# Two transformer blocks on one core: the norms at the ends of the projections rearranged between PE, DVE and ACT

## The chip, the cores and the metric

The kernel runs on one core of a Trainium2 chip. The metric is the device time of one execution in microseconds, the median of three runs.

## What is computed

512 tokens of 1024 features go through two decoders in turn, each of two layers, all in float32. Cut to what the change touches:

```python
def rmsnorm(x, g):
    y = x * lax.rsqrt(jnp.mean(x * x, axis=-1, keepdims=True) + 1e-6)
    return y * g

# first decoder: two layers, then a closing norm
h = h + mixer(rmsnorm(h, norm1[i]), ...)          # attention, then @ w_out
h = h + conv_ffn(rmsnorm(h, ffn_norm[i]), ...)    # gelu(conv(g)) * u, then @ w_out
x = rmsnorm(h, final_norm)

# second decoder: two layers with a norm before and behind each half
mix = merged @ w_out[l]
x = x + rmsnorm(mix, norm_mix_post[l])
f = conv_gated_mlp(rmsnorm(x, norm_ffn_pre[l]), ...)
x = x + rmsnorm(f, norm_ffn_post[l])
```

The mixers are block, differential, dilated and latent attention in the first decoder, and axial attention, pooling and neighbourhood attention, gated and merged, in the second.

## The kernel before

**Layout.** Activations lie transposed: features on the 128 partitions, 512 tokens along the row, so the state `x` is eight tiles of 128x512. [...]

**Products.** Each float32 weight and activation is split into a high and a low part in `fp32r`; a product is three matmuls (L470 to L472: high by high, high by low, low by high). The high part of a normed `x` is `hh`, the rest is `hl`, both without the factor 1/rms: that factor multiplies the results (`rs`, 128x512, or `rsT`, one column per 128 tokens). GpSimd (POOL) splits the weights ahead of TensorE: a cast to `wh` (L450) and a subtraction for `wl` (L452), two buffers deep, fed by SyncE's DMAs.

**Order.** Every engine runs its own list, written by hand; semaphores join them, with counts worked out ahead by `counts` and `starts`. Output tiles of a projection go to the PSUM banks PA and PB in turn; bank PA is used again one tile later, once `pa_taken` has been raised.

**The end of a projection** has two forms.

- *out0, down0, out1, down1* (`x_add`, L1606): DVE adds the bank to the tile of `x` (L1613), which frees the bank; ACT makes `hh` from `x` times the next gain (L1040) and the square in `tmp` (L1041); DVE makes `hl` (L1298) and adds the square to `acc` (L1304). The norms before `up0` and `up1` are summed late, inside the next projection (`sum_acc`, one 128x512 product of ones with `acc`).
- *out2, down2* (`mix_copy`): ACT squares the bank (L1053), DVE copies it to `mix` (L1622) and adds the square (L1304).

**The five places where TensorE waits** are `norm_final` behind down1, and `norm_mp` and `norm_fp` behind out2 and down2 in each of two layers (I number the layers 0 and 1). `stat` (L506) sums `acc` over partitions into four columns of tokens (L511, four products of 2 columns each), ACT takes the root (L1027), DVE inverts it (L1277) and multiplies it into an identity, which gives 128x512 in `acc` (`factor`, L1278), and TensorE spreads it with a product of ones with that matrix (`spread`, L519) into bank O0. Then DVE renews `x` tile by tile: in `norm_post` with L1336 (`mix` by gain by O0), L1338 (the sum), in `norm_final` with L1325; ACT makes `hh` and the square, DVE `hl` (L1298), and TensorE starts the next projection tile by tile as `hl` comes: `up2` (`up` with `squared`), or `axial_kv` (L915 to L917 and PB), both with a 128x512 sum of ones with each square (L502). `moba_v` and `mla_cq` use `stat` and `spread` too, between products of a value projection.

Of the kernel before, what the change touches and what calls it, by code (L numbers as in the profile page):

```python
# [60 lines left out]
def counts(kind, seg=None, fin=0, mix=0):  # L61
    c = dict(e=SEGMENTS[seg][0] if seg else 0, a=0, b=0, u=0, g=0, v=0, n=fin, k=0, s=0, q=0, h=0, x=0, z=0,
             m=0, d=fin, r=0, st=0, df=0, pl=0, dr=0, dc=0)
    if kind == "x_in":
        c.update(s=1 + DT, q=DT, h=DT)
    elif kind == "v":
        c.update(v=1)
# [9 lines left out]
    elif kind == "mla_cq":  # L77
        c.update(a=1, b=1, d=fin)
# [4 lines left out]
    elif kind == "norm_post":  # L83
        c.update(q=DT, h=DT, x=DT, d=fin + DT)
# [49 lines left out]
    ("up1", counts("up1", "up1")), ("down1", counts("out", "down1")),  # L134
# [55 lines left out]
def build(nc, x_in, weights, consts, cols_in, lam_in, rel_in, rpb_in, strips_rel, strips_na, out):  # L190
    with ExitStack() as ctx:
# [110 lines left out]
        diag_ready, spread_ready = sem("diag_ready"), sem("spread_ready")  # L302
# [160 lines left out]
        def _(pe):  # L463
# [42 lines left out]
            def stat(b, spread_now=True):  # L506

                pe.wait_ge(acc_done, b["s"])
                pe.wait_ge(o_taken, b["u"] + 2)
                for t in range(QT):  # L510
                    last = mm(O1[:, 2 * t:2 * t + 2], acc[:, t * P:t * P + P], ones[:, 0:2], start=True, stop=True)  # L511
                last.then_inc(st_ready, 1)
                if spread_now:
                    spread(b)

            def spread(b):

                pe.wait_ge(diag_ready, b["n"] + 1)
                mm(O0[:, :], ones[:, :], acc[:, :], start=True, stop=True).then_inc(spread_ready, 1)  # L519
# [451 lines left out]
            def moba_stat():  # L971
                pe.wait_ge(table_in, 16 * NTABLE)
                stat(H("moba_v"), False)
# [14 lines left out]
            stat(b, False)  # L988
# [12 lines left out]
            stat(H("norm_final"))  # L1001
            with pe.Fori(0, LAYERS2) as l:
# [14 lines left out]
        def _(act):  # L1017
# [25 lines left out]
            def renew_out(b, gain_at, e_per=1):  # L1043

                with act.Fori(0, 4) as i:
                    for j, (bank, taken, key) in enumerate(((PA, pa_taken, "a"), (PB, pb_taken, "b"))):
                        if gain_at is None:
                            act.wait_ge(entry_done, b["e"] + e_per * (2 * i + j + 1) + 2)
                        else:
                            act.wait_ge(taken, b[key] + i + 2)  # L1050
                        act.wait_ge(acc_done, b["s"] + 2 * i + j + 1 - j)
                        if gain_at is None:
                            A(tmp[j][:, :], bank[:, :], ACT.Square).then_inc(sq_ready, 1)  # L1053
                        else:
                            renew(2 * i + j, gain_at, tmp[j][:, :])
# [938 lines left out]
```

## Time and profile before

| | us |
|---|---|
| median of 3 runs (lowest, highest) | 3264.05 (3263.01, 3266.23) |
| the profiled execution | 3260.93 |
| its span, first to last instruction | 3259.1 |
| TensorE busy (share) | 3105.8 (95%) |
| POOL busy | 1660.0 (51%) |
| DVE busy | 1481.7 (45%) |
| ACT busy | 788.6 (24%) |

A busy share of TensorE counts a matmul also while it waits in the pipeline or runs at half clock. The idle stretches lie at a few places; the timeline shows them, and the windows show the clock in them. The profiled execution is 1.8 us longer than its span and 3.1 us below the median.

### The profile page before, as it was taken

Reading aid. Unit: us, or ns where it says so; the run is one execution under the profiler, and the core shown is the slowest. Engines: PE = TensorE matmul, PEld = TensorE weight load, DVE = VectorE, ACT = ScalarE, POOL = GpSimd, SP = SyncE. Lnnn points to the kernel's source line nnn. Section 1 sums busy time; section 2 is a strip of 40 time slices with the busy share of each in tenths; the row PEclk is TensorE's granted clock in tenths of the full one; section 3 lists DMA queues with packets and bytes.
Section 4 is the critical chain, followed back from the end, with each engine's and each line's share of the span. In section 5 each row is a group of like instructions: output and inputs, shape, how many; then the busy total and the mean of one; then the engine's idle time right before and its main releaser. Section 6 shows DMA issues by size and latency. Waiting matters only on the chain.

```text
span 3259.1 us, 44842 instructions
## 1 busy us (share of the span) xinstructions
PE 3105.8 (95%) x14594; PEld 2441.7 (75%) x14594; DVE 1481.7 (45%) x2555; ACT 788.6 (24%) x1425; POOL 1660.0 (51%) x1254
## 2 busy tenths in 40 slices
PE   8998999999899999899999989998899999989997
PEld 6776888876678887667678868887667678868885
DVE  3246444332454433633533476631633433576622
ACT  2343221014322211243421122210142511122201
POOL 4324666662166666312346646665313256646674
PEclk9999999999999999889999989999889999999998
DMA  6251223321022233102312222232102322212232
GB/s 159 78 161 65 94 95 105 105 91 59 26 90 97 97 109 104 36 23 57 93 68 97 87 66 97 96 114 85 40 33 62 75 78 97 90 65 97 97 113 74
DMA packets 99595, 274.79 MB, mean 84 GB/s; under 512 B 38126, under 2 KB 38894, under 8 KB 99490
## 3 DMA queue, kind: packets, MB, share of 16 engines
q1 hardware_dynamic: 97328, 269.07, 25.8%
q10 hardware_dynamic: 2162, 4.36, 0.7%
q8 instruction: 61, 1.00, 0.1%
q14 instruction: 44, 0.36, 0.0%
HBM read 269.66 MB, written 11.54 MB: 86 GB/s over the span
## 4 chain that ended last, share of the span: by engine, by line
PE 71%; DVE 4%; issue 2%; ACT 1%; DVEq 0%; ACTq 0%
PE PA L470 11%; PE PA L471 10%; PE PA L472 10%; PE PB L470 8%; PE PB L472 8%; PE PB L471 8%; PE T L598 2%; PE O L604 2%; PE S L567 2%; PE O L699 1%; PE S L660 1%; PE O L502 1%; DVE hl L1298 1%; DVE tmps L1336 0%; PE PB L759 0%
## 5 line engine op out<-in xcount | busy, mean ns | idle before, releaser
L452 POOL TENSOR_TENSOR wl<-raw,wh 128x1024 fp32r<-128x1024 f32 (+2 forms) x416 | 1126.6, 2708 | 33.4
L449 POOL TENSOR_TENSOR zero<-zero 128x1 f32<-128x1 f32 x416 | 82.7, 199 | 1530.7 <-PE PA L472 799.0
L470 PE MATMUL PA<-hh,wh 128*128 128x512 f32 x1392 | 566.2, 407 | 30.4 <-DVE hl L1298 11.4
L471 PE MATMUL PA<-hl,wh 128*128 128x512 f32 x1392 | 550.1, 395 | 0.0
L472 PE MATMUL PA<-hh,wl 128*128 128x512 f32 x1392 | 549.6, 395 | 0.0
L450 POOL CAST wh<-raw 128x1024 fp32r<-128x1024 f32 (+2 forms) x416 | 476.8, 1146 | 0.0
L470 PEld LDWEIGHTS PA<-hh,wh 128*128 128x128 f32 x1392 | 265.7, 191 | 139.8 <-issue 65.8
L470 PE MATMUL PB<-hh,wh 128*128 128x512 f32 x896 | 358.5, 400 | 0.0
L472 PE MATMUL PB<-hh,wl 128*128 128x512 f32 x896 | 350.4, 391 | 0.0
L471 PE MATMUL PB<-hl,wh 128*128 128x512 f32 x896 | 350.2, 391 | 0.0
L472 PEld LDWEIGHTS PA<-hh,wl 128*128 128x128 f32 x1392 | 266.3, 191 | 57.6
L471 PEld LDWEIGHTS PA<-hl,wh 128*128 128x128 f32 x1392 | 266.4, 191 | 54.0 <-issue 2.2
L1074 ACT ACTIVATE probs<-biased,stats 128x512 f32<-128x512 f32 (+2 forms) x240 | 155.2, 647 | 408.6 <-PE T L598 226.3
L1631 DVE SCALAR_TENSOR_TENSOR tmps<-S,cols,tmps 128x511 f32<-128x511 f32 (+1 forms) x264 | 197.9, 750 | 39.6 <-DVE tmps L1631 19.8
L470 PEld LDWEIGHTS PB<-hh,wh 128*128 128x128 f32 x896 | 169.1, 189 | 47.5 <-issue 14.4
L472 PEld LDWEIGHTS PB<-hh,wl 128*128 128x128 f32 x896 | 168.7, 188 | 36.0
L471 PEld LDWEIGHTS PB<-hl,wh 128*128 128x128 f32 x896 | 169.1, 189 | 33.7 <-issue 1.2
L598 PEld LDWEIGHTS T<-ident,probs 128*128 128x128 f32 x792 | 98.8, 148 | 72.5 <-issue 37.3
L1170 ACT ACTIVATE T<-tmps 128x512 f32<-128x512 f32 x88 | 53.0, 602 | 391.7 <-DVE tmps L1631 391.7
L1298 DVE SCALAR_TENSOR_TENSOR hl<-x,cols,hh 128x512 fp32r<-128x512 f32 (+1 forms) x80 | 129.3, 1622 | 39.0 <-ACT hh L1040 38.8
L470 PE MATMUL PA<-acth,wh 128*128 128x512 f32 x352 | 137.4, 390 | 0.0
L598 PE MATMUL T<-ident,probs 128*128 128x128 f32 x792 | 136.3, 288 | 0.8 <-ACT probsT L1080 0.8
(285 smaller groups left out, 4928.0 us busy)
## 6 DMA issues: line engine op xcount, KB each, us to landing
raw<-in_w_up SPq DMA_DIRECT2D x176, 512.0 KB, 3.4
raw<-in_w_down SPq DMA_DIRECT2D x64, 768.0 KB, 4.2
raw<-in_w_merge SPq DMA_DIRECT2D x48, 768.0 KB, 4.2
raw<-in_w_out SPq DMA_DIRECT2D x32, 512.0 KB, 3.4
strips_na<-in_rpb SPq DMA_DIRECT2D x1, 7620.0 KB, 32.0
raw<-in_w_pool SPq DMA_DIRECT2D x12, 512.0 KB, 3.4
raw<-in_w_na_qk SPq DMA_DIRECT2D x12, 512.0 KB, 3.5
raw<-in_w_na_v SPq DMA_DIRECT2D x8, 512.0 KB, 3.5
```

Source lines behind the costliest of these rows:

```text
L449: nc.gpsimd.tensor_tensor(zero[:, :], zero[:, :], zero[:, :], ALU.add)
L450: nc.gpsimd.tensor_copy(wh[s][:, 0:width], raw[s][:, 0:width]).then_inc(w_head, 1)
L452: nc.gpsimd.tensor_tensor(wl[s][:, 0:width], raw[s][:, 0:width], wh[s][:, 0:width].bitcast(F), ALU.subtract).then_inc(w_split, 1)
L470: mm(dst, h_, rh, start=first, stop=False)
L471: mm(dst, h_, rl, start=False, stop=False)
L472: return mm(dst, l_, rh, start=False, stop=last)
L567: mm(SB[t % 2][:, 0:L], q_sb[r, qt * P:qt * P + P], k_sb[r, 0:L], start=True, stop=True).then_inc(s_ready, 1)
L598: last = nc.tensor.transpose(TB[t % 2][:, k * P:k * P + P], probs[t % 2][:, k * P:k * P + P], ident[:, :])
L604: last = mm(OB[t % 2][:, 0:dv], probsT[t % 2][:, k * P:k * P + P], values(k), start=(k == 0), stop=(k == L // P - 1))
L1074: A(probs[t % 2][:, 0:L], biased[t % 2][:, 0:L], ACT.Exp, scale=-1.0, bias=mn[:, t % 8:t % 8 + 1], accum_out=den[:, t % 8:t % 8 + 1]).then ...
L1298: STT(out=tile(hl, j), in0=tile(x, j), scalar=cols[:, bass.ds(gain_at + j, 1)], in1=tile(hh, j).bitcast(F), op0=ALU.mult, op1=ALU.subtract ...
L1631: ins = STT(out=dst[:, lo:hi], in0=src[:, lo - d:hi - d], scalar=w(k), in1=dst[:, lo:hi], op0=ALU.mult, op1=ALU.add)
```

## The change

1. **Late norms** (norm_final, norm_mp, norm_fp). `stat_last` takes the place of `stat`: TensorE sums `acc`, which now holds seven squares only, and then adds the eighth straight from `tmp[1]` into the same PSUM columns. `x_sum` and `mix_copy` leave out DVE's last addition.
2. **Factor and spreading** (all seven uses). DVE only inverts; the multiplication into an identity is gone. `spread` is four products of 128 columns, whose stationary operand is a column of `rsT` repeated 128 times, and whose moving one is the identity.
3. **Products that nothing reads** (`turning`, 128x512, identity by `causal`, into bank T0): (1, 1, 2) in norm_final, (0, 1, 3) in the others, before the last square, before the spreading and behind it.
4. **The sum in its bank** (out0, down0, out1). DVE adds `x` into the bank; `hh`, `hl` and the square are made from the bank, and ACT copies the bank to `x` at the end. Only that copy frees the bank.
5. **down1** no longer makes `hh` and `hl`; the squares are of `x` (`x_sum`, `square_out`).
6. The 128x512 sums inside `up0`, `up1`, `up2` and `axial_kv` stay.

```diff
 def counts(kind, seg=None, fin=0, mix=0):
...
-        c.update(a=4, b=4, s=1 + DT, q=DT, h=0 if mix else DT)
+        c.update(a=4, b=4, s=DT if mix else 1 + DT, q=DT, h=0 if mix else DT, xs=0 if mix else DT)
...
-    ("up1", counts("up1", "up1")), ("down1", counts("out", "down1")),
+    ("up1", counts("up1", "up1")), ("down1", counts("out", "down1", mix=1)),
...
+            def token_sums(src, first, last):
+
+                for t in range(QT):
+                    out_ = mm(O1[:, 2 * t:2 * t + 2], src[:, t * P:t * P + P], ones[:, 0:2], start=first and t == 0,
+                              stop=last and t == QT - 1)
+                if last:
+                    out_.then_inc(st_ready, 1)
...
+            def turning(times):
+
+                for _ in range(times):
+                    mm(T0[:, :], ident[:, :], causal[:, :], start=True, stop=True)
+
+            def stat_last(b, turns):
+
+                pe.wait_ge(acc_done, b["s"])
+                pe.wait_ge(o_taken, b["u"] + 2)
+                token_sums(acc, True, False)
+                turning(turns[0])
+                pe.wait_ge(sq_ready, b["q"])
+                token_sums(tmp[1], False, True)
+                turning(turns[1])
+                spread(b)
+                turning(turns[2])
+
+            def spread(b):
+
+                pe.wait_ge(inv_ready, b["n"] + 1)
                 for t in range(QT):
-                    last = mm(O1[:, 2 * t:2 * t + 2], acc[:, t * P:t * P + P], ones[:, 0:2], start=True, stop=True)
-                last.then_inc(st_ready, 1)
-                if spread_now:
-                    spread(b)
-
-            def spread(b):
-
-                pe.wait_ge(diag_ready, b["n"] + 1)
-                mm(O0[:, :], ones[:, :], acc[:, :], start=True, stop=True).then_inc(spread_ready, 1)
+                    last = mm(O0[:, t * P:t * P + P], rsT[:, t:t + 1].to_broadcast([P, P]), ident[:, :], start=True, stop=True)
+                last.then_inc(spread_ready, 1)
...
-            stat(H("norm_final"))
+            stat_last(H("norm_final"), (1, 1, 2))
...
-                stat(H("norm_mp", l))
+                stat_last(H("norm_mp", l), (0, 1, 3))
...
-                stat(H("norm_fp", l))
+                stat_last(H("norm_fp", l), (0, 1, 3))
...
+            def renew_out(b, gain_at):
+
+                with act.Fori(0, 4) as i:
+                    for j, (bank, taken) in enumerate(((PA, pa_taken), (PB, pb_taken))):
+                        n = 2 * i + j
+                        act.wait_ge(xs_ready, b["xs"] + n + 1)
+                        A(tile(hh, n), bank[:, :], ACT.Copy, scale=cols[:, bass.ds(gain_at + n, 1)]).then_inc(hh_ready, 1)
+                        act.wait_ge(h_ready, b["h"] + n + 1)
+                        act.wait_ge(acc_done, b["s"] + 2 * i + 1)
+                        A(tmp[j][:, :], bank[:, :], ACT.Square).then_inc(sq_ready, 1)
+                        A(tile(x, n), bank[:, :], ACT.Copy).then_inc(taken, 1)
...
             def factor(b):
 
-                chain_at(b["d"])
                 dve.wait_ge(std_ready, b["n"] + 1)
-                link(v.reciprocal(rsT, rsT))
-                TT(acc[:, :].rearrange("p (t n) -> p t n", t=QT),
-                   ident[:, :].rearrange("p (a n) -> p a n", a=1).to_broadcast([P, QT, P]),
-                   rsT.rearrange("p (t a) -> p t a", a=1).to_broadcast([P, QT, P]), ALU.mult).then_inc(diag_ready, 1)
+                v.reciprocal(rsT, rsT).then_inc(inv_ready, 1)
...
                 clear(b)
                 with dve.Fori(0, 4) as i:
+                    for j, bank in enumerate((PA, PB)):
+                        n = 2 * i + j
+                        dve.wait_ge(entry_done, b["e"] + e_per * (n + 1) + 2)
+                        TT(bank[:, :], tile(x, n), bank[:, :], ALU.add).then_inc(xs_ready, 1)
+                        dve.wait_ge(hh_ready, b["h"] + n + 1)
+                        STT(out=tile(hl, n), in0=bank[:, :], scalar=cols[:, bass.ds(gain_at + n, 1)],
+                            in1=tile(hh, n).bitcast(F), op0=ALU.mult, op1=ALU.subtract).then_inc(h_ready, 1)
+                        add_squares(b, n, tmp[j][:, :])
+
+            def x_sum(b, e_per):
...
+                        TT(tile(x, n), tile(x, n), bank[:, :], ALU.add).then_inc(taken, 1)
+                        if j < adds:
+                            add_squares(b, n, tmp[j][:, :])
+
+                with dve.Fori(0, 3) as i:
+                    both(i, 2)
+                both(3, 1)
```

The order of TensorE's list at `norm_fp`, behind the last product of down2 (`acth` by `wl` into bank PB; O is O1 in the narrow sums, O0 in the spreading; T is T0; `stats` holds `rsT`; a number after x repeats the row). Before:

```order
L472 MATMUL PB<-acth,wl 128x512
L855 REGISTER_ALU
L855 COMPARE_AND_BRANCH
L508 REGISTER_ALU
L511 MATMUL O<-ones,acc 128x2 [waits o_taken,acc_done]
L511 MATMUL O<-ones,acc 128x2 x3
L519 MATMUL O<-acc,ones 128x512 [waits diag_ready]
```

With the change (line numbers of the new file):

```order
L878 COMPARE_AND_BRANCH
L527 REGISTER_ALU
L509 MATMUL O<-ones,acc 128x2 [waits o_taken,acc_done]
L509 MATMUL O<-ones,acc 128x2 x3
L531 REGISTER_ALU
L509 MATMUL O<-ones,tmps 128x2 [waits sq_ready]
L509 MATMUL O<-ones,tmps 128x2 x3
L523 MATMUL T<-causal,ident 128x512
L541 MATMUL O<-ident,stats 128x128 [waits inv_ready]
L541 MATMUL O<-ident,stats 128x128 x3
L523 MATMUL T<-causal,ident 128x512 x3
```

The narrow sums are now eight products with the second wait in their middle, and four products that nothing reads stand around the spreading. `norm_mp` has the same rows; `norm_final` has one such product ahead of the second wait too, and two at the end.

ACT's list in the loop of out0, one tile (bank PA). Before:

```order
L1051 ISA [waits pa_taken]
L1040 ISA [waits acc_done]
L1040 REGISTER_ALU
L1040 ACTIVATE hh<-x,cols 128x512
L1041 ACTIVATE tmps<-x 128x512
```

With the change:

```order
L1072 ISA [waits xs_ready]
L1072 ACTIVATE hh<-PA,cols 128x512
L1073 REGISTER_ALU
L1074 REGISTER_ALU [waits h_ready]
L1075 ACTIVATE tmps<-PA 128x512 [waits acc_done]
L1076 REGISTER_ALU
L1076 ACTIVATE x<-PA 128x512
```

ACT reads the bank three times instead of `x` twice, the second time only behind DVE's `hl`, and the bank is free when the third is done.

## Rows read from the trace of the kernel before

**Rows 1.** The page, part 2: TensorE clock granted in 40 slices of 81.5 us, tenths

```profile
PEclk9999999999999999889999989999889999999998
```

**Rows 2.** Timeline at the first norm_mp: start us, us, engine, line, out<-in [idle before]

```profile
1881.91 0.60 ACT L1053 ACTIVATE tmps<-PB 128x512 f32<-128x512 f32 x1 [4.69 <-PE PB L472]
...
1882.53 1.28 ACT L1027 ACT_TABLE_LOAD   x1
...
1883.27 2.82 DVE L1304 TENSOR_TENSOR acc<-acc,tmps 128x512 f32<-128x512 f32 x1
...
1886.15 1.86 PE L511 MATMUL O<-ones,acc 128*128 128x2 f32 x8 [4.27 <-DVE acc L1304]
...
1888.05 0.26 ACT L1027 ACTIVATE stats<-O,eps 128x4 f32<-128x4 f32 x1 [4.24 <-PE O L511]
...
1889.31 2.07 PE L519 MATMUL O<-acc,ones 128*128 128x512 f32 x2 [1.29 <-DVE acc L1278]
...
1891.55 0.75 DVE L1336 SCALAR_TENSOR_TENSOR tmps<-mix,cols,O 128x512 f32<-128x512 f32 x1 [2.30 <-PE O L519]
...
1895.13 0.79 PE L470 MATMUL PA<-hh,wh 128*128 128x512 f32 x1 [3.75 <-DVE hl L1298]
...
1907.41 0.50 PE L470 MATMUL PA<-hh,wh 128*128 128x512 f32 x1 [0.18 <-DVE hl L1298]
```

**Rows 3.** Windows after norm_fp, layer 0: PE, PEld, DVE, ACT, POOL busy, PEclk, DMA

```profile
2279.10:2294.00 14.90, 14.90 (x50) 12.16 (x50) 12.69 (x19) 8.04 (x14) 0.00 (x0) 0.50 0.01 4
```

**Rows 4.** Timeline at norm_final, last tile of down1 to the next projection

```profile
1296.79 0.72 ACT L1040 ACTIVATE hh<-x,cols  x1 [13.63 <-DVE x L1613]
...
1305.82 1.41 DVE L1325 SCALAR_TENSOR_TENSOR x<-x,cols,O 128x512 f32<-128x512 f32 x2 [2.17 <-PE O L519]
...
1308.24 0.47 PE L915 MATMUL S<-wh,hh 128*128 128x128 f32 x1 [2.46 <-DVE hl L1298]
...
1335.57 0.79 PE L470 MATMUL PA<-hh,wh 128*128 128x512 f32 x1
```

**Rows 5.** Timeline after norm_fp of layer 0: first product of axial_kv, first of pool

```profile
2279.10 0.47 PE L915 MATMUL S<-wh,hh 128*128 128x128 f32 x1 [3.81 <-DVE hl L1298]
...
2309.00 0.79 PE L470 MATMUL PA<-hh,wh 128*128 128x512 f32 x1
```

**Rows 6.** Timeline of two products on PB, five 128-row blocks apart, at full clock

```profile
1319.06 0.45 PE L470 MATMUL PB<-hh,wh 128*128 128x512 f32 x1
...
1333.52 0.45 PE L470 MATMUL PB<-hh,wh 128*128 128x512 f32 x1
```

**Rows 7.** Timeline at the last norm_fp: end of down2, start of the renewal

```profile
3234.08 0.60 ACT L1053 ACTIVATE tmps<-PB 128x512 f32<-128x512 f32 x1 [14.21 <-PE PB L472]
...
3241.57 0.75 DVE L1336 SCALAR_TENSOR_TENSOR tmps<-mix,cols,O 128x512 f32<-128x512 f32 x1 [2.29 <-PE O L519]
```

**Rows 8.** Timeline at full clock: the narrow statistics (mla_cq) and a 128x512 sum (up1)

```profile
678.81 0.95 PE L511 MATMUL O<-ones,acc 128*128 128x2 f32 x8
...
940.88 1.02 PE L497 MATMUL O<-acc,ones 128*128 128x512 f32 x2
```

**Rows 9.** Timeline: a table load and the activation behind it, dilated attention

```profile
732.79 1.28 ACT L1074 ACT_TABLE_LOAD   x1 [4.76 <-DVE stats L1375]
...
734.09 0.40 ACT L1074 ACTIVATE probs<-biased,stats 128x128 f32<-128x128 f32 x1
```

**Rows 10.** Two lines: ns min/median/max, first and last start, forms

```profile
L1658 DVE TENSOR_TENSOR T<-T,tmps x88: 699/700/700, 323.2 to 3118.0; 128x512 f32<-128x512 f32 x88
...
L1304 DVE TENSOR_TENSOR acc<-acc,tmps x64: 677/680/2880, 270.5 to 3235.4; 128x512 f32<-128x512 f32 x64
```

**Rows 11.** Timeline: two tiles of out1 on bank PA, DVE

```profile
905.15 0.69 DVE L1613 TENSOR_TENSOR x<-x,PA 128x512 f32 x1 [0.71 <-PE PA L472]
...
907.05 2.23 DVE L1298 SCALAR_TENSOR_TENSOR hl<-x,cols,hh  x1 [1.21 <-ACT hh L1040]
...
916.04 0.69 DVE L1613 TENSOR_TENSOR x<-x,PA 128x512 f32 x1 [0.71 <-PE PA L472]
```

More of the change, by code:

```diff
@@ L66, in counts @@
     elif kind == "v":
-        c.update(v=1)
+        c.update(v=1, f=fin)
     elif kind == "q0":
@@ L972, in moba_stat @@
                 pe.wait_ge(table_in, 16 * NTABLE)
-                stat(H("moba_v"), False)
+                stat(H("moba_v"))
             v_projection(H("moba_v"), between=(None, moba_stat, lambda: spread(H("moba_v"))))
@@ L1225, in _ @@
             renew_out(H("out1"), CAT["ffn_norm1"])
-            sum_root(H("up1")); up(H("up1"), ACT.Gelu); renew_out(H("down1"), CAT["final"])
+            sum_root(H("up1")); up(H("up1"), ACT.Gelu); square_out(H("down1"), 2, True)
             b = H("norm_final")
@@ L1330, in norm_post @@
                 factor(b)
+                chain_at(b["d"])
                 dve.wait_ge(spread_ready, b["n"] + 1)
@@ new lines, in x_sum, with both @@
+            def x_sum(b, e_per):
+                clear(b)
+                def both(i, adds):
+                    for j, (bank, taken) in enumerate(((PA, pa_taken), (PB, pb_taken))):
+                        n = 2 * i + j
+                        dve.wait_ge(entry_done, b["e"] + e_per * (n + 1) + 2)
+                        TT(tile(x, n), tile(x, n), bank[:, :], ALU.add).then_inc(taken, 1)
[4 more added lines that the diff above has]
+                both(3, 1)
@@ L1617, in mix_copy, with both @@
             def mix_copy(b):
                 clear(b)
-                with dve.Fori(0, 4) as i:
+                def both(i, adds):
                     for j, (bank, taken) in enumerate(((PA, pa_taken), (PB, pb_taken))):
-                        dve.wait_ge(sq_ready, b["q"] + 2 * i + j + 1)
-                        v.tensor_copy(tile(mix, 2 * i + j), bank[:, :]).then_inc(taken, 1)
-                        add_squares(b, 2 * i + j, tmp[j][:, :])
+                        n = 2 * i + j
+                        dve.wait_ge(sq_ready, b["q"] + n + 1)
+                        v.tensor_copy(tile(mix, n), bank[:, :]).then_inc(taken, 1)
+                        if j < adds:
+                            add_squares(b, n, tmp[j][:, :])
@@ L1625, in conv @@
+                with dve.Fori(0, 3) as i:
+                    both(i, 2)
+                both(3, 1)
             def conv(dst, src, col, taps, last):
@@ L1796, in _ @@
             x_add(H("out1"), 1, CAT["ffn_norm1"])
-            up(H("up1"), CAT["conv1"], False); x_add(H("down1"), 2, CAT["final"])
+            up(H("up1"), CAT["conv1"], False); x_sum(H("down1"), 2)
             norm_final(H("norm_final"), CAT["final"], CAT["mix_pre"])
```

41 lines of the change are left out of this document (17 added, 24 removed).

## The prediction

> **What bounds the kernel now.** I read first the page: TensorE is busy for 95% of the span, POOL for 51%, DVE for 45%, so time is won only where TensorE stands idle or runs slowly. Its granted clock comes next [rows 1]: most slices read 9, six read 8; of these, counted from 0, 16 holds `norm_final`, 23 the first `norm_mp`, 28 follows the first `norm_fp`, and 39 is the end. So two things can be bought: shorter idle stretches, and a clock that does not fall.
>
> Then the timeline at the first `norm_mp` [rows 2]. I count from E, the start of ACT's square of the last tile (1881.91), since nothing before it changes. The square takes 0.60, but DVE's addition of it takes 2.82. The same form takes 0.68 in most of its uses and up to 2.88 [rows 10]: both its operands lie in SBUF, and while POOL subtracts, it is held. After it come the narrow sums (1.86, at half clock), the root (0.26), 1.00 from the root's end to the spreading (1889.31 less 1888.31: inverse and diagonal), the spreading (2.07, half clock), a hop of 0.17, and DVE begins the renewal at 1891.55. **E to renewal is 9.64 us**, three such places alike (both `norm_mp` and the first `norm_fp`), each with a product waiting behind it.
>
> What is gained there counts only if what follows is not itself bound otherwise. In `norm_mp` TensorE is still waiting for DVE's `hl` at 1907.41 [rows 2], 12.28 us after its first product: DVE renews a tile in three instructions of some 0.7 each, and seven further tiles come at its pace. The whole train moves forward with its start; a better clock adds nothing. In `norm_final` and the first `norm_fp` each tile is followed by a block of 15 products and a square's sum. At full clock a block takes (1333.52 − 1319.06) / 5 = **2.89 us** [rows 6], more than DVE's three instructions, so TensorE's clock sets the pace. But the clock there was 0.50 for 14.90 us, with TensorE busy throughout [rows 3]. Here both a start and a clock can be won.
>
> **The change, part by part.**
>
> *Chain of the late norms.* TensorE sums the seven other squares in the shade of the last square, then that square itself: full-clock price of all narrow products 0.95 [rows 8], so from E + 0.65 to E + 1.60. DVE's 2.82, with its hold, drops out. Now the table load ends last: it begins 0.62 after E and takes 1.28 [rows 2], to E + 1.90. The root (0.26) ends at E + 2.2 with the hop. Of the 1.00 behind it some 0.70 was the diagonal, a 128x512 DVE instruction like that of [rows 10]; 0.30 stays, E + 2.5. The spreading is now four products of 128 columns with their own loads. No row shows this form. Below, it is bounded by the eight narrow products (0.95), above by four times the one wide sum (4.1) [rows 8]; I take the wide sum's 1.02, since the columns are as many and the loads of the narrow products cost little. E + 3.5, with the hop E + 3.65. **Gain 9.64 − 3.65 = 6.0, three times: 18.0.**
>
> *norm_final.* ACT's copy `hh` (at 1296.79) is gone, so the square begins there. Renewal at 1296.79 + 3.65 = 1300.4 instead of 1305.82 [rows 4]: **5.5**.
>
> *The last norm_fp* (nothing behind it but DVE's renewal and the stores; DVE was not held here): 3241.57 − 3234.08 = 7.5 [rows 7], now 3.65: **3.8**.
>
> *The clock.* It fell because TensorE, between the last product of the projection and the first of the next (over 13 us), worked for 3.9 us (1.86 and 2.07 [rows 2]). After the change that stretch is E + 3.65 and the 3.6 from renewal to first product [rows 2], some 7.3 us, and holds 0.95 + 1.02 + 3 x 1.02 of products beside one more ahead of the spreading: about 6 us of work, with no pause over 1.2 us. I take it to hold at 2.4 GHz. Then eight blocks cost 8 x 2.89 = 23.1 us. `norm_final` took 1335.57 − 1308.24 = 27.3 [rows 4]: **4.2**. The first `norm_fp` took 2309.00 − 2279.10 = 29.9 [rows 5]: **6.8**. At half clock these products would cost double, and the three last (3 x 2.07) would run past the first product by 2.6 us in `norm_fp`.
>
> *Unread product ahead of the spreading*: starts at E + 1.60, done by E + 2.62, 0.1 behind the inverse; inside the rounding. Those behind the spreading: three of 1.02 in 3.6 us, two in `norm_final`, where renewal to first product is 2.42 (1308.24 − 1305.82 [rows 4]). Nothing waits.
>
> *Factor of `moba_v` and `mla_cq`.* The diagonal goes from DVE, TensorE has the same columns. Both lie between products of a projection: 0.
>
> *Sum in its bank* (out0, down0, out1). Nothing ends earlier: TensorE reaches each next bank by its own products. The cost is the hold. Before, the bank was free after 0.69; DVE's `hl` could be held to 2.23 [rows 11]. Now: 1.90 from the addition to the start of `hl` (907.05 − 905.15 [rows 11]), `hl` 0.75, a hop of 0.2, square 0.60, copy 0.60: 4.05. `hl` reads a bank and SBUF; the same kind of operands took 699 or 700 ns in all of 88 uses [rows 10], so it isn't held. The bank has 10.89 for two tiles [rows 11], so 5.44 until the next product of its own. **0.** If `hl` were held after all, 4.05 + 1.5 = 5.5: up to 0.3 for each of 17 reuses (three loops; the first use of each finds its bank free). At down1 two instructions of ACT and DVE go, hidden behind tiles twice as long: 0, but for the copy counted above.
>
> **Sum:** 18.0 + 5.5 + 3.8 + 4.2 + 6.8 = 38.3. The profiled execution took 3260.93 (1.8 us more than its span); 3260.9 − 38.3 = 3222.6. The median lies 3.1 us higher; by that, **3225.7**.
>
> *Where page and trace differ.* The table load is the longest link of the new chain. In [rows 9] one starts at 732.79 and its activation at 734.09, 1.30 later, and I took that. The Trainium skill (ScalarE activation tables: per-element evaluation and per-set limits, on the cost of ACT_TABLE_LOAD) adds a drain of about 1.38 us behind the load. By that rule, with a root 1.38 later at five places, an estimate of 3225.7 + 6.9 = 3232.6 results; this trace disagrees with it.
>
> **Rivals.**
>
> 1. *The clock falls in the holes anyway.* For it: the pauses for the square and the root remain, and the stretch at 0.50 shows how readily it fell. Against: TensorE works most of the stretch. Lost are 4.2 + 6.8 = 11.0, a second 1.05 for each of five spreadings (5.3), and 2.6 + 1.7 where late unread products delay the first block: (3 x 2.07 − 3.6, and 2 x 2.07 − 2.42): 20.6. **3246.3.** If only one of the two blocks' clocks is saved: about 3232.
> 2. *The spreading is dearer than one wide sum.* At its upper bound 3.1 more for each of five: 15.5, **3241**. For it: each of four products loads a weight matrix made of a repeated column, a read no row shows. Against: eight narrow products with eight loads need 0.95.
> 3. *The bank is held too long: slower.* If TensorE waits for each of the 17 reuses, the loss is 17 x (h − 5.44), h being the hold. It passes the 38.3 gained plus 6.5 (0.2%) from h = 8.1; at 8.3, 49 us are lost, **3275**. It needs ACT or DVE to be held for 4 us beyond the 4.05. For it: `hh`, `hl`, square and copy now form one line for each bank, in turn on two engines. Against: none of these forms took over 2.3 in out1.
> 4. *A mild hold*, h = 5.8: 6 us, **3232**.
> 5. *The root comes late behind its table load.* In the chain before, ACT waited 4.24 for the sums [rows 2], so that chain can't show how soon a root may follow its load; now nothing lies between. If it needed as long again as the load (1.28), five times: 6.4, **3232**. Against: [rows 9].
>
> **Chances.** Forecast (within 4 us of 3225.7) 0.55; one clock term lost, 3232: 0.15; rival 1: 0.12; rival 2 or partly so: 0.03; mild hold: 0.04; late root: 0.03; no gain to speak of, by parts that cancel: 0.03; slower: 0.05. The low end takes in other stretches at half clock [rows 1], such as the 14.90 us of [rows 3], which cost up to 7 us each and may fall otherwise once everything behind them moves: 3218. The high end takes in rival 1: 3246. A difference under 0.2% (6.5 us) can't be told from none here. Faster by more: 0.92; within: 0.03; slower: 0.05.
>
> **What the profile after must show.** From the last square's start to the renewal 3.6 to 3.8 us at each of five places, with the root straight behind its table load; the narrow sums at about 1 us, the four products of the spreading at about 1. PEclk above 0.9 behind `norm_final` and the first `norm_fp`, and some 23 us for their eight blocks. No wait on `pa_taken` or `pb_taken` in out0, down0, out1, and `hl` there at 0.75 throughout. Wrong it would be if the clock reads 0.5 behind the holes, if TensorE pauses at the head of each tile of out0, or if the spreading takes over 2 us at full clock.

## The result, and where the time went

| | before | with the change |
|---|---|---|
| median of 4 runs, us (lowest, highest) | 3265.14 (3263.01, 3266.23) | 3227.76 (3222.63, 3228.72) |
| ratio, 95% interval | | 0.9882 (0.9870 to 0.9894) |
| the profiled execution | 3260.93 | 3222.63 |
| its span; mean granted clock | 3259.1; 0.969 | 3220.5; 0.982 |

The kernel is 37.4 us faster, where 38.3 was forecast. The median lies 2.1 us above the 3225.7 of the forecast (range 3218 to 3246). For the profiled execution the forecast's sum gave 3222.6, and 3222.63 was measured. That last agreement is partly luck, as the balance below shows.

The page after, parts 1 and 2 (engine totals, clock in 40 slices of 80.5 us), to be read against [rows 1]:

```profile
PE 3101.5 (96%) x14716; PEld 2438.9 (76%) x14716; DVE 1420.2 (44%) x2535; ACT 796.3 (25%) x1441; POOL 1661.9 (52%) x1254
...
PEclk9999999999999999999999999999899999999999
```

The slices 16, 17, 23, 29 and 39 now read 9; the only 8 left is in slice 28 (from 2254). TensorE's busy time hardly moved (3105.8 to 3101.5): most unread products lie in time that it stood idle, and the products behind them are shorter because the clock stayed up.

The chain at the first `norm_mp`, with the change, answers to [rows 2]:

```profile
1867.26 0.60 ACT L1087 ACTIVATE tmps<-PB 128x512 f32<-128x512 f32 x1 [4.69 <-PE PB L472]
...
1867.88 1.28 ACT L1050 ACT_TABLE_LOAD   x1
...
1867.91 1.05 PE L509 MATMUL O<-ones,tmps 128*128 128x2 f32 x8
...
1869.17 0.26 ACT L1050 ACTIVATE stats<-O,eps 128x4 f32<-128x4 f32 x1
...
1869.47 0.18 DVE L1308 RECIPROCAL stats<-stats 128x4 f32<-128x4 f32 x1 [0.89 <-ACT stats L1050]
...
1869.77 1.09 PE L541 MATMUL O<-ident,stats 128*128 128x128 f32 x8
...
1870.69 2.74 PE L523 MATMUL T<-causal,ident 128*128 128x512 f32 x6
...
1871.02 0.75 DVE L1365 SCALAR_TENSOR_TENSOR tmps<-mix,cols,O 128x512 f32<-128x512 f32 x1 [1.37 <-PE O L541]
...
1874.59 0.50 PE L470 MATMUL PA<-hh,wh 128*128 128x512 f32 x1 [1.16 <-DVE hl L1326]
```

(Here the trace has two instructions for a product: x8 are four products, x6 three.) From the last square (1867.26) to the renewal (1871.02) it is 3.76 us instead of 9.64. The narrow sums of the last square are done by 1868.96 while the table is still loading, until 1869.16; the root starts at 1869.17, and the spreading is 1.09 long. The load is the link that ends last, by 0.2. The other places: 3.67 at `norm_final`, 3.75 to 3.77 at the rest.

The renewal and the first products at `norm_final` and the first `norm_fp`, with the first product of the pooling stage (compare [rows 4] and [rows 5]):

```profile
1296.91 0.63 ACT L1087 ACTIVATE tmps<-x 128x512 f32 x1 [14.26 <-DVE x L1656]
...
1300.58 1.41 DVE L1353 SCALAR_TENSOR_TENSOR x<-x,cols,O 128x512 f32<-128x512 f32 x2 [1.25 <-PE O L541]
...
1303.00 0.32 PE L938 MATMUL S<-wh,hh 128*128 128x128 f32 x1 [0.74 <-DVE hl L1326]
...
1325.90 0.80 PE L470 MATMUL PA<-hh,wh 128*128 128x512 f32 x1
```

```profile
2252.66 0.32 PE L938 MATMUL S<-wh,hh 128*128 128x128 f32 x1 [1.24 <-DVE hl L1326]
...
2275.55 0.80 PE L470 MATMUL PA<-hh,wh 128*128 128x512 f32 x1
```

The eight blocks take 22.90 and 22.89 us instead of 27.33 and 29.90. The same 14.90 us as in [rows 3] (columns as there):

```profile
2252.66:2267.56 14.90, 14.89 (x94) 12.30 (x95) 14.70 (x19) 8.05 (x14) 3.86 (x3) 1.00 0.01 3
```

The granted clock is 1.00 where it was 0.50, and TensorE issued 94 instructions in the stretch where it had issued 50.

The balance of the two profiled executions, by the landmarks of these rows (last square, renewal, first product, first product of the pooling stage):

| stretch | forecast | before less after |
|---|---|---|
| start to the last tile of down1 | 0 | −0.2 |
| `norm_final`, last tile to renewal | 5.5 | 5.5 |
| its eight blocks (clock) | 4.2 | 4.4 |
| pooling stage to the last square of out2, layer 0 | 0 | **+5.0** (546.34 to 541.36) |
| `norm_mp` twice, first `norm_fp` | 18.0 | 17.6 (3 x 5.88) |
| blocks behind the first `norm_fp` (clock) | 6.8 | 7.0 |
| pooling stage to the last square of out2, layer 1 | 0 | **−4.5** (541.16 to 545.65) |
| last `norm_fp` | 3.8 | 3.7 |
| all (span 3259.1 to 3220.5) | 38.3 | 38.6 |

Two terms of 5 us that nobody forecast cancel. They lie in a stage that the change doesn't touch. The windows over that stage, layers 0 and 1, first before, then with the change (columns as in [rows 3], the clock third from the end):

```profile
1335.57:1881.91 546.34, 528.51 (x2578) 400.25 (x2576) 241.73 (x429) 147.99 (x283) 233.95 (x167) 0.95 0.23 69
2309.00:2850.16 541.16, 521.99 (x2578) 395.80 (x2576) 241.43 (x429) 147.80 (x283) 233.92 (x167) 0.97 0.23 69
```

```profile
1325.90:1867.26 541.36, 522.48 (x2581) 396.44 (x2579) 241.54 (x429) 147.80 (x284) 233.94 (x167) 0.97 0.23 69
2275.55:2821.20 545.65, 525.93 (x2581) 398.09 (x2579) 241.75 (x429) 147.90 (x283) 234.61 (x167) 0.96 0.23 69
```

The longer passes are those with the lower granted clock, which falls in other places in each execution. I come back to them in the experiment on the pooling stage. A reading of the forecast that held: from the renewal at `norm_mp` to the next last square it is 374.2 to 374.3 us in both kernels, so there only the earlier start counts, not the clock.

In out0 the bank is held for 3.7 us from DVE's addition (266.60) to the end of ACT's copy (270.31), where 4.05 was forecast, and once it shows (DVE's `hl`, the copy that frees the bank, the next product on it):

```profile
268.36 0.75 DVE L1644 SCALAR_TENSOR_TENSOR hl<-PA,cols,hh 128x512 f32 x1 [1.06 <-ACT hh L1072]
...
269.72 0.59 ACT L1076 ACTIVATE x<-PA 128x512 f32 x1
...
270.45 0.79 PE L470 MATMUL PA<-yh,wh 128*128 128x512 f32 x1 [3.32 <-ACT x L1076]
```

### The profile page after: what moved, and what is told of

Read it like the earlier page. It is cut to its first block, busy times and chain, and to the rows that moved or that the text cites. A ratio compares the mean times of both kernels' runs of the same rounds, so it can differ in the third digit from the quotient of the medians.

```text
span 3220.5 us, 45047 instructions
## 1 busy us (share of the span) xinstructions
PE 3101.5 (96%) x14716; PEld 2438.9 (76%) x14716; DVE 1420.2 (44%) x2535; ACT 796.3 (25%) x1441; POOL 1661.9 (52%) x1254
## 4 chain that ended last, share of the span: by engine, by line
PE 71%; DVE 3%; issue 2%; ACT 1%; DVEq 0%; ACTq 0%
PE PA L470 11%; PE PA L471 10%; PE PA L472 10%; PE PB L470 8%; PE PB L471 8%; PE PB L472 8%; PE T L621 2%; PE O L627 2%; PE S L590 2%; PE O L722 1%; PE S L683 1%; PE O L502 1%; DVE strip L1756 0%; DVE tmps L1365 0%; DVE hl L1326 0%
## 5 line engine op out<-in xcount | busy, mean ns | idle before, releaser
L471 PE MATMUL PA<-actl,wh 128*128 128x512 f32 x352 | 137.0, 389 | 0.0
L472 PE MATMUL PA<-acth,wl 128*128 128x512 f32 x352 | 136.9, 389 | 0.0
```

Of the source, the lines that this page charges most:

```text
L471: mm(dst, h_, rl, start=False, stop=False)
L472: return mm(dst, l_, rh, start=False, stop=last)
```

## The experiments

Each label names a kernel, made from the changed one unless the text says otherwise. The times are medians of four runs (dve_sum: five), the ratios are to the kernel before, and each trace is of one execution. The eight runs of the changed kernel and of `control`, which is the same kernel, spread from 3222.6 to 3229.1. Every run of no_unread, unread_only, dve_sum and six_copies lies above that, every run of pool_fill and combined below it. The runs of the other five kernels overlap with it, so their medians alone prove little, and I read each effect at its place in the trace. "Chain" is from the last square's start to the renewal, in the order `norm_final`; `norm_mp`, `norm_fp` of layer 0; the same of layer 1. "Blocks" are the eight blocks behind `norm_final` and the first `norm_fp`. The hole is the stretch between TensorE's last product of one projection and its first of the next.

| kernel | median | chain | blocks |
|---|---|---|---|
| before (`norm_final` from the square at 1297.42) | 3265.1 | 8.40; 9.64, 9.63; 9.65, 7.49 | 27.3, 29.9 |
| changed | 3227.8 | 3.67; 3.76, 3.75; 3.77, 3.75 | 22.9, 22.9 |
| control | 3227.4 | 3.67; 3.77, 3.75; 3.77, 3.75 | 22.9, 22.9 |
| no_unread | 3236.6 | 4.59; 4.67, 4.67; 4.69, 4.67 | 30.1, 28.0 |
| ahead_only | 3229.7 | 3.67; 3.75, 3.75; 3.77, 3.75 | 22.9, 26.9 |
| behind_only | 3230.2 | 4.58; 4.68, 4.66; 4.68, 4.67 | 23.9, 22.9 |
| unread_only (from the kernel before) | 3246.4 | 7.66; 8.83, 9.49; 8.93, 5.90 | 22.9, 22.9 |
| dve_sum | 3253.7 | 7.91; 8.94, 9.75; 9.49, 6.06 | 22.9, 22.9 |
| old_spread | 3234.6 | 4.57; 6.48, 5.52; 5.53, 4.45 | 22.9, 22.9 |
| sum_in_x | 3223.1 | 3.67; 3.76, 3.75; 3.76, 3.75 | 22.9, 22.9 |
| six_copies | 3234.3 | 3.67; 3.76, 3.76; 3.76, 3.75 | 22.9, 22.9 |
| early_table | 3226.3 | 4.29; 4.39, 4.38; 4.39, 4.38 | 22.9, 22.9 |
| pool_fill | 3220.3 | 3.67; 3.76, 3.75; 3.77, 3.75 | 22.9, 22.9 |
| combined | 3217.8 | 4.29; 4.38, 4.37; 4.39, 4.38 | 22.9, 22.9 |

### Do the unread products hold the clock, or does the shorter hole?

**no_unread**

```diff
-            stat_last(H("norm_final"), (1, 1, 2))
+            stat_last(H("norm_final"), (0, 0, 0))
...
-                stat_last(H("norm_mp", l), (0, 1, 3))
+                stat_last(H("norm_mp", l), (0, 0, 0))
```

(`norm_fp` likewise.) Expected:

> The changed kernel with all unread products taken out (0, 0, 0 at every late norm). Theory A, the unread products hold the clock: it reads 0.5 behind norm_final and the first norm_fp again, the eight blocks there take 27 and 30 us instead of 22.9 each, and with some spreadings at half clock the time goes up by 11 to 15 us, to 3239 to 3243. Rival B, the shorter hole alone holds the clock: the blocks stay at 22.9 and the time within 2 us of 3227.8.

Measured 3236.6, ratio 0.9907 (0.9890 to 0.9923): a little below the range I gave. At the first `norm_fp`, the spreading and the renewal, and the windows behind it and behind `norm_final`:

```profile
2257.93 2.07 PE L541 MATMUL O<-ident,stats 128*128 128x128 f32 x8 [0.73 <-DVE stats L1308]
...
2260.16 0.75 DVE L1365 SCALAR_TENSOR_TENSOR tmps<-mix,cols,O 128x512 f32<-128x512 f32 x1 [2.28 <-PE O L541]
```

```profile
2263.81:2278.71 14.90, 14.90 (x64) 12.59 (x65) 12.69 (x19) 8.04 (x14) 0.00 (x0) 0.64 0.01 3
1307.14:1322.04 14.90, 14.90 (x50) 12.15 (x50) 8.55 (x13) 8.09 (x14) 0.00 (x0) 0.50 0.00 1
```

The spreading is back at 2.07, half clock, and the blocks at 0.64 and 0.50. In this execution theory A holds in its parts: 0.9 in each chain, 7.2 and 5.1 us in the blocks, 16.9 us by place, and the two profiled executions differ by 16.2. The medians differ by 8.9 only. The three other runs have no trace, so where they were faster isn't shown.

**unread_only** leaves the long hole as it was and only puts unread products into it:

```diff
+            def turning(times):
+                for _ in range(times):
+                    mm(T0[:, :], ident[:, :], causal[:, :], start=True, stop=True)
...
-            stat(H("norm_final"))
+            stat(H("norm_final"), turns=(3, 1, 2))
```

(in `stat`: ahead of the wait for `acc`, ahead of the spreading, behind it; (3, 1, 3) in `norm_mp` and `norm_fp`.)

> The kernel before, with unread products added at the five late norms and nothing else: three ahead of the wait for the sum in acc, one ahead of the spreading, two or three behind it. Theory A: the clock stays at full speed, both sets of eight blocks take 22.9 (11.4 us less), and the narrow sums and the spreading halve (1.9 us at each of five places, 9 us): about 3245. Rival B, only the length of the hole counts: no more than 3 us from 3265.

Measured 3246.4, ratio 0.9941 (0.9924 to 0.9957). The window behind the first `norm_fp`:

```profile
2268.96:2283.86 14.90, 14.90 (x94) 12.29 (x95) 14.70 (x19) 8.05 (x14) 3.87 (x3) 1.00 0.01 3
```

The blocks are at full clock with the chain in the hole still 7.7 to 9.5 us long ahead of them. So the work in the hole decides, not its length alone, and the unread products alone win back 11.4 us of blocks. The chains gained less than the 1.9 us forecast: 0.1 at the first `norm_fp`, 0.7 or 0.8 at three places, 1.6 at the last. At the first `norm_fp` the three products ahead of the sum are over while DVE's addition is still held; behind the sums the unread product takes 2.05, half clock, and the spreading starts only behind it:

```profile
2255.61 2.74 PE L509 MATMUL T<-causal,ident 128*128 128x512 f32 x6
...
2257.17 2.82 DVE L1312 TENSOR_TENSOR acc<-acc,tmps 128x512 f32<-128x512 f32 x1
...
2261.39 2.05 PE L509 MATMUL T<-causal,ident 128*128 128x512 f32 x2
...
2263.24 1.91 PE L527 MATMUL O<-acc,ones 128*128 128x512 f32 x2
```

**ahead_only** and **behind_only** split them:

```diff
-            stat_last(H("norm_final"), (1, 1, 2))
+            stat_last(H("norm_final"), (1, 1, 0))
...
-                stat_last(H("norm_mp", l), (0, 1, 3))
+                stat_last(H("norm_mp", l), (0, 1, 0))
```

```diff
-            stat_last(H("norm_final"), (1, 1, 2))
+            stat_last(H("norm_final"), (0, 0, 2))
...
-                stat_last(H("norm_mp", l), (0, 1, 3))
+                stat_last(H("norm_mp", l), (0, 0, 3))
```

> The changed kernel with only the unread products ahead of the spreading, (1, 1, 0) and (0, 1, 0). With all of them the spreading runs at full clock (last square to renewal 3.76, eight blocks 22.9), with none at half (4.67, blocks 28 to 30). Theory A1, a product is needed ahead of each pause: renewal at 3.76, but the 2.4 and 3.6 us behind the spreading are then empty and the clock falls there, blocks 26 to 28, time 3235. Rival A2, the one ahead suffices: blocks 22.9, time 3228.

> The changed kernel with only the unread products behind the spreading, (0, 0, 2) and (0, 0, 3). Theory A1: the clock is already down at the spreading (last square to renewal 4.67), the products behind run at half clock and the first block is late by up to 2; blocks 24 to 28; time 3237 to 3240. Rival, those behind suffice: the clock is up again by the first product, blocks 22.9 and time 3231.

Measured 3229.7 (ratio 0.9895, 0.9878 to 0.9911; runs 3225.7 to 3234.2) and 3230.2 (0.9888, 0.9871 to 0.9904; runs 3226.1 to 3234.9). Windows behind `norm_fp` and `norm_final` with only those ahead, then with only those behind:

```profile
2258.07:2272.97 14.90, 14.90 (x67) 12.40 (x68) 12.69 (x19) 8.05 (x14) 0.66 (x2) 0.71 0.01 3
1304.95:1319.85 14.90, 14.90 (x94) 12.30 (x95) 8.54 (x13) 8.09 (x14) 3.54 (x3) 1.00 0.01 1
```

```profile
2263.43:2278.33 14.90, 14.90 (x95) 12.30 (x95) 14.70 (x19) 8.05 (x14) 3.86 (x3) 1.00 0.01 3
1306.75:1321.65 14.90, 14.90 (x88) 11.84 (x86) 8.55 (x13) 8.10 (x14) 3.54 (x3) 0.95 0.01 1
```

In these traces each group has its own job. Those ahead keep the spreading at full clock (3.75 against 4.67), and behind `norm_final`, with 2.42 from renewal to first product, that is enough. Behind `norm_fp`, with 3.65, it isn't: 0.71, blocks 26.9. Those behind cannot save the spreading, but the blocks start at full clock or get there soon (1.00 and 0.95, 23.9 us). A1 was too gloomy in three points: the blocks of behind_only, those behind `norm_final` in ahead_only, and the late first block, which didn't come: with half the clock at the spreading, behind_only's first products still start 2.42 and 3.66 us behind the renewal, as before. Its median lies 7 us below A1's range.

### What the last square's sum and the diagonal were worth

**dve_sum** lets DVE add all eight squares; TensorE sums `acc` once:

```diff
-                token_sums(acc, True, False)
-                turning(turns[0])
-                pe.wait_ge(sq_ready, b["q"])
-                token_sums(tmp[1], False, True)
+                token_sums(acc, True, True)
...
```

(DVE's two loops take in the eighth tile again. The unread product ahead of the last square in `norm_final` goes as well.)

> The changed kernel, but DVE adds the eighth square to acc again and TensorE sums acc once. By the theory that DVE's held addition was the main link, the last square to the renewal takes 3.3 us more (7.1 instead of 3.76) at both norm_mp and the first norm_fp, and 1.3 more at norm_final and the last norm_fp, where the addition is not held: 12.5 us in all, 3240; if the clock falls too in the longer holes, 3251. Rival, the table load hides the sum: 3228.

Measured 3253.7 (ratio 0.9964, 0.9950 to 0.9979; single runs 3239 to 3255). The addition at the first `norm_mp`, then the unread product and the spreading at the first `norm_fp`, then the addition at `norm_final`:

```profile
1871.78 2.83 DVE L1329 TENSOR_TENSOR acc<-acc,tmps 128x512 f32<-128x512 f32 x1
```

```profile
2259.45 2.05 PE L523 MATMUL T<-causal,ident 128*128 128x512 f32 x2
...
2261.30 1.91 PE L538 MATMUL O<-ident,stats 128*128 128x128 f32 x8
```

```profile
1298.71 2.34 POOL L452 TENSOR_TENSOR wl<-raw,wh 128x1024 fp32r<-128x1024 f32 x1
...
1299.10 2.50 DVE L1329 TENSOR_TENSOR acc<-acc,tmps 128x512 f32<-128x512 f32 x1 [0.89 <-ACT tmps L1084]
```

The chain is longer by 5.2 to 6.0 at three places, where I had said 3.3, and by 4.2 at `norm_final` and 2.3 at the last, where I had said 1.3: 23.4 us in all, and the median lies above both my figures. The held addition returned with its 2.83, and the longer pause let the clock fall in the hole: the unread product took 2.05 and kept the spreading back until 2261.30, though the inverse had been there since 2260.10, and the spreading took 1.91. At `norm_final` the addition is held as well (2.50), because without `hh` it now starts while POOL subtracts. The part is worth more than its own duration, since it also keeps the pause short. The blocks of the profiled execution (3239.1, the lowest of five) are at full clock; those of the slower ones weren't seen. That execution lies only 16.4 above the changed kernel's, because its two passes through the pooling stage took 538.9 and 539.6, 8.6 less in all.

**old_spread** puts back the diagonal and the single wide product:

```diff
-                for t in range(QT):
-                    last = mm(O0[:, t * P:t * P + P], rsT[:, t:t + 1].to_broadcast([P, P]), ident[:, :], start=True, stop=True)
-                last.then_inc(spread_ready, 1)
+                mm(O0[:, :], ones[:, :], acc[:, :], start=True, stop=True).then_inc(spread_ready, 1)
```

and in `factor` the multiplication of the identity into `acc`.

> The changed kernel with the old factor and spreading (DVE multiplies into an identity, TensorE one 128x512 product). The diagonal's 0.69 comes back on the path at five places, the spreading itself costs 1.02 instead of 1.09: 3 us more, last square to renewal 4.4, time 3231. Rival, the four products with a repeated column are dearer than they look and give that back: no difference at any of the five places.

Measured 3234.6 (ratio 0.9898, 0.9881 to 0.9914). POOL's subtraction and DVE's diagonal at the first `norm_fp`, the spreading at the first `norm_mp`, and the diagonal there in the kernel before:

```profile
2256.82 2.34 POOL L452 TENSOR_TENSOR wl<-raw,wh 128x1024 fp32r<-128x1024 f32 x1
...
2257.95 1.77 DVE L1308 TENSOR_TENSOR acc<-ident,stats 128x512 f32<-128x512 f32 x1
```

```profile
1879.05 2.07 PE L540 MATMUL O<-acc,ones 128*128 128x512 f32 x2 [1.57 <-DVE acc L1308]
```

```profile
1888.56 0.69 DVE L1278 TENSOR_TENSOR acc<-ident,stats 128x512 f32<-128x512 f32 x1
```

At three of five places the diagonal takes 1.77 instead of 0.69 (0.90 at `norm_final`), since both its operands lie in SBUF and in the short chain it falls into POOL's subtraction; in the kernel before, it came after it. At one of them the spreading had half the clock too, which makes 6.48, and at the first `norm_fp` the late unread products hold up the first product by another 0.7. By place the old form costs 0.90, 2.72, 1.77, 1.76 and 0.70 in the chains, 7.9 us where I expected 3. The four products with a repeated column cost 1.09 against 1.02: the bound of 4.1 in my rival was far off.

### The sum in its bank

**sum_in_x**

```diff
-                        TT(bank[:, :], tile(x, n), bank[:, :], ALU.add).then_inc(xs_ready, 1)
...
+                        TT(tile(x, n), tile(x, n), bank[:, :], ALU.add).then_inc(taken, 1)
+                        remainder(b, n, gain_at)
```

(`remainder` makes `hl` from `x`) and ACT makes `hh` and the square from `x`.

> The changed kernel with the old x_add at out0, down0 and out1: DVE adds into x and frees the bank at once, ACT makes hh and the square from x. By the forecast (hold 3.8 us against 5.4 between two uses of a bank) nothing changes: 3226 to 3231, and no wait of TensorE in out0 and out1 in either kernel. Rival, the sum in its bank wins time by DVE's shorter hl (0.75 instead of 2.2 to 2.3): then this kernel is 5 us slower or more.

Measured 3223.1 (ratio 0.9866, 0.9850 to 0.9883), below the range I gave; its runs (3218.6 to 3226.5) overlap with those of the changed kernel. What TensorE waits for in out0:

```profile
270.00 0.79 PE L470 MATMUL PA<-yh,wh 128*128 128x512 f32 x1 [3.03 <-POOL wl L452]
```

With the sum in `x` that product waits 3.03 for POOL's weights; with the sum in its bank 3.32 for the copy. So the wait that the trace shows for the sum in its bank costs 0.3 us, at one place: out0's first two tiles end within a us of each other (TensorE idles for 3.32 until 270.45, so from 267.13, and DVE's first addition started at 266.60), and bank PA is wanted again at once. DVE's `hl`, 2.1 to 3.9 in these loops from `x`, fell to 0.75 and nothing came of it. Whether the sum in its bank costs more than the 0.3 stays open: the median here is 4.7 below the changed kernel's, and combined, which has the sum in `x` too, is lower than its other two edits explain. No wait in the traces accounts for it.

**six_copies**

```diff
+                        for c in range(more):
+                            A((mh, ml)[j][:, c, :], bank[:, :], ACT.Copy)
                         A(tile(x, n), bank[:, :], ACT.Copy).then_inc(taken, 1)
```

with `more` 6 in out0 and out1.

> The changed kernel with six more copies of the bank by ACT (into buffers that nothing reads) ahead of the one that frees it, in out0 and out1. The trace of the changed kernel has 3.67 us from the addition to the end of that copy; each more adds 0.5, so the hold is 6.7. If a bank has 5.44 us between its uses and every reuse pays the rest, TensorE waits 1.3 us at 12 to 14 reuses, 16 to 18 us in all, 3245. If a wait on one bank gives the other its time, only every second reuse pays: 8 to 10 us, 3237. Rival, the hold is not what TensorE would wait for: no change.

Measured 3234.3 (ratio 0.9903, 0.9886 to 0.9919). What TensorE waited for in out0 and its surroundings (264 to 320), and in out1 (886 to 960): us in total, times, longest.

```profile
PE PA L470 <- ACT x L1078: 10.4, 4, 6.3
```

```profile
PE PA L470 <- ACT x L1078: 5.5, 4, 1.5
```

Four waits in each loop, 15.9 us, of which 3.3 are there without the copies: 12.6 us, between my two figures for the sum (the median rose by 6.5, the profiled execution by 12.2). Only bank PA is waited for: a wait on it gives PB the time it lacks, so every second reuse pays, the fourth being the first product of the next projection. In out1 each costs 1.3 to 1.5: the hold there is 6.6 from the addition's start to the last copy's end (941.11 to 947.72), against 5.44, with a hop. In out0 the first is 6.25.

### The table load, the pooling stage, and both

**early_table**

```diff
+                A(spare[:, :], eps[:, 0:1], ACT.Sqrt)
...
-            stat_last(H("norm_final"), (1, 1, 2))
+            stat_last(H("norm_final"), (2, 0, 2))
```

(and (1, 0, 3) for the others; the root of one column stands at the head of `square_out`.)

> The changed kernel with a root of one column (into a buffer that nothing reads) at the head of the last projection, so that the table load runs while ACT is idle, and the unread product between the sums and the spreading moved ahead of the last square: (2, 0, 2) and (1, 0, 3). In the trace of the changed kernel the load ends 1.93 us after the last square's start and the narrow sums 1.74. If the load is the last link, the renewal comes 0.2 earlier (3.55) at five places, 1 us in all: 3226.5. Rival, the rule of a drain behind the load: more than 1 us at each place, 3221. If the clock falls without the product between the sums and the spreading: 4.4 us instead of 3.55, 3231.

Measured 3226.3 (ratio 0.9881, 0.9865 to 0.9898), the chain **longer**, 4.38. By place that is 3.1 us more at five places, so the median agrees with my 3226.5 by chance. Unread product, sums and root at the first `norm_fp`:

```profile
2252.54 1.10 PE L524 MATMUL T<-causal,ident 128*128 128x512 f32 x2
...
2253.49 0.95 PE L510 MATMUL O<-ones,tmps 128*128 128x2 f32 x8
...
2254.47 0.26 ACT L1051 ACTIVATE stats<-O,eps 128x4 f32<-128x4 f32 x1 [1.94 <-PE O L510]
```

The table load is gone from the chain, but I had moved the unread product to where TensorE is busy: it starts at 2252.54, straight behind the sums of `acc` and 0.01 after the square's end, and the sums of the last square wait for it until 2253.49. A miss in the design, which still shows that the clock holds with the product ahead of the last square (spreading 1.16). What the early load is worth it doesn't show; in the changed kernel's trace the load was the last link by 0.2. The version with the early table and the product behind the sums wasn't run.

**pool_fill** puts nine unread products into the pooling stage, identity by `causal` into bank O0; `fill(n)` issues n of them:

```diff
-                pool_u(1); turn_rotate(kv["b"] + 1, kv["r"], tmp[2])
-                pool_u(2); pool_u(3)
+                pool_u(1); fill(4); turn_rotate(kv["b"] + 1, kv["r"], tmp[2])
+                pool_u(2); fill(1); pool_u(3); fill(2)
...
-                q_sum(ax["b"], ax["r"]); turn_rotate(ax["b"], ax["r"], qr_sb)
+                q_sum(ax["b"], ax["r"]); fill(1); turn_rotate(ax["b"], ax["r"], qr_sb); fill(1)
```

> The changed kernel with nine unread products more in the pooling stage of each of the two axial layers, where TensorE waits for DVE and ACT (longest 4.4 us) and the clock falls three times for 17 us in all behind it. If unread products hold it there as in the late norms, most of these stretches read 1.0, and of 34 us at half clock in two layers a part comes back: 3 to 8 us, 3220 to 3225. Rival, TensorE is not the bound in that stage: the clock stays up and the time doesn't move.

> The changed kernel unaltered, to see on the same chip as the three others how much its time and its low-clock stretches vary: 3222 to 3229, chains of 3.76 (3.67 at norm_final), blocks of 22.9.

pool_fill took 3220.3 (3217.5 to 3221.0; ratio 0.9862, 0.9846 to 0.9879), the control on the same chip 3227.4 (3223.9 to 3229.1; 0.9881, 0.9864 to 0.9897): 7.1 us, and no single run of one in the range of the other. Windows over the pooling stage and the first axial attention of layers 0 and 1, first the control, then pool_fill:

```profile
1327.34:1420.00 92.66, 81.27 (x318) 56.61 (x317) 54.72 (x92) 26.05 (x48) 25.74 (x26) 0.83 0.11 34
2280.56:2373.00 92.44, 79.55 (x309) 54.61 (x308) 54.24 (x90) 24.75 (x46) 26.39 (x26) 0.83 0.11 35
```

```profile
1327.43:1420.00 92.57, 87.90 (x347) 58.36 (x346) 55.80 (x94) 27.67 (x51) 27.86 (x29) 0.91 0.11 35
2275.47:2368.00 92.53, 86.91 (x344) 58.71 (x343) 55.83 (x94) 27.57 (x51) 27.00 (x28) 0.91 0.11 35
```

The mean clock in them rose from 0.83 to 0.91 in both layers. From the pooling stage's first product to the last square of out2 the control took 544.9 and 545.7 us, pool_fill 539.8 and 540.7. The changed kernel's profiled execution took 541.4 and 545.7, and the kernel before 546.3 and 541.2, with the same instructions. This is where the two stray terms of the balance come from, and probably a good part of why a kernel's single runs lie 6 us apart.

The control's two passes were among the slow ones, though, so the pair of traces overstates the gain. In the twelve kernels without this filling, all with the same instructions in that stage, 24 passes took 538.9 to 546.3 us, 543.0 in the mean; the four passes of pool_fill and combined took 536.0 to 540.7, 538.9 in the mean. That is 4.1 us less for a pass and 8 for two, in line with the 7.1 of the medians, and the granted clock, 0.984 or 0.985 in all four runs of pool_fill against 0.980 or 0.981 in the control's, says the same.

**combined** is sum_in_x with both edits above.

> The changed kernel with x_add as in the kernel before (sum in x), the early table load, and the unread products of the pooling stage. If the parts add up: 0.3 us for the wait at out0 that goes, 1 for the table, 3 to 8 for the clock: 3218 to 3223. Rival, only noise between them: 3227.

Measured 3217.8 (3213.0 to 3221.2; ratio 0.9857, 0.9841 to 0.9873), 9.6 below the control, not told apart from pool_fill. Its chains carry early_table's 0.6 us each, so by its parts (0.3 and 7.1 gained, 3.1 lost) it should be 4.3 below; the other 5 us have no cause that a run shows. It has the lowest median of this study.

## Why the prediction was right, and where it was not

- **The chain, 6.0 us a place.** Right: 5.88. The working (table load as the last link, sums in its shade, 0.30 for the inverse, 1.02 for the spreading) was off by 0.1 in the spreading, the product ahead of it included.
- **norm_final, 5.5.** Right, 5.5, though the working's own 1305.82 less 1300.4 is 5.4. Counted from the last tile's addition, the square began 0.82 later, where I had put it at 0.92.
- **The clock, 4.2 and 6.8.** Right, 4.4 and 7.0, and no_unread and unread_only show that the products do it. That the two groups do different jobs I had not said. Rival 1's 1.05 for each spreading came out as 0.9 in no_unread; its 2.6 and 1.7 for late unread products didn't appear in behind_only.
- **The rule on the table load.** The Trainium skill (ScalarE: Activation LUTs, What ACT_TABLE_LOAD costs) adds a drain of about 1.38 us to the load at each switch of the table set. The prediction gives this rule under another page's title. Here the load ended at 1869.16 and the root began at 1869.17; the trace disagrees, and rival 5 falls.
- **Factor and spreading.** The price of the new form was right. The value of the old one's removal was sized on the old timing (0.70); in the new chain the diagonal would be held, 1.77 at three places. It changes nothing in the sum, since the diagonal is gone either way, but whoever had kept it would have been surprised.
- **The sum in its bank, 0.** Wrong by 0.3 at one place, and the working had a flaw: "17 reuses" counted down0, whose tiles last 14.9 us, and made every reuse pay; three loops of eight tiles with the first use of each of two banks free are 18, besides. Two loops are at risk, and every second reuse pays. So my slower case would have needed a hold far over 8.1. The sign "no wait on `pa_taken`" failed at that one place.
- **Nothing else moves.** This failed, by +5.0 and −4.5 us. I had put 7 us of it into the range. The median lies 2.1 above the forecast and 5.1 above the profiled execution, where before it lay 3.1 above, or 4.2 by all four runs: a profiled execution is one draw of such stretches.

## What to carry to other kernels

A dependent chain between two busy stretches of TensorE costs its length and, when it lets the clock fall, more in the products behind it (here 4.4 and 7.0 us behind chains of 8.4 and 9.6): count both, and check first that the stage behind is bound by TensorE. Take each link of the chain out of the engine that another one can hold, and put work into the pauses on both sides of it; such work must not stand in front of a product that is waited for, least of all at half clock. And sum the parts against one profiled execution, stage by stage, since a stage that no edit touched differed by up to 7.5 us from one execution to the next.

## What the runs showed of the hardware

- The same stage, instruction for instruction, took 538.9 to 546.3 us in 24 passes of twelve kernels; in the four compared above the longer ones had the lower mean granted clock (0.95 and 0.96 against 0.97).
- DVE was held by POOL's subtraction (2.34 us at the late norms) where both its operands are in SBUF: the addition took 2.50 to 2.83 instead of 0.68, the diagonal 1.77 instead of 0.69. With one operand in a bank it wasn't: `hl` took 0.75 in all 24 uses of the changed kernel, each within one of POOL's subtractions.
- An activation started 0.01 us behind the end of its table load, at all five late norms of the changed kernel.
- Products whose stationary operand is one column repeated 128 times cost little more than a wide one with a full operand: four of 128 columns took 1.09 us, one of 512 columns 1.02.
